# Strassen's seven products for pairs of up projections in a hybrid decoder trunk

## The chip, the cores and the metric

The kernel runs on one core of a Trainium2 chip. The metric is the device time of one execution in microseconds (us); lower is better. TensorE is called PE, its weight loads PEld, VectorE is DVE, ScalarE is ACT, GpSimd is POOL and SyncE is SP.

## What is computed

Two layers (`DEPTH`), 256 tokens, width 1024, hidden width 2816, float32. Each layer is

```python
x = x + 0.5 * swiglu(rmsnorm(x, norm_ffn1), w1, w3, w2)     # first FFN
h = rmsnorm(x, norm_mix); P = h @ w_in                       # the mixer: three branches, gates, one output
x = x + merged(retention, window attention, memory attention) @ w_o
x = x + 0.5 * swiglu(rmsnorm(x, norm_ffn2), w1, w3, w2)     # second FFN
...
def swiglu(h, w1, w3, w2):
    return (jax.nn.silu(h @ w1) * (h @ w3)) @ w2
```

and a final RMS norm. The memory attention projects `mem` (256 tokens, normed) in every layer, at the start of the mixer.

## The kernel before

**Matmuls in three passes.** Every large product is made from two-part operands: a value is split into a high part in the type fp32r and a low part, the rest. `three_passes` (L442 to L444) issues low x high, high x high and high x low into one PSUM bank, each with a stationary tile of 128 activations x 128 tokens and 512 moving columns of weight.

**Weights.** All large weights come from HBM as a stream of 1 MB units of 128x2048, in the order of use; 123 units per layer: 33 for each FFN, 57 for the mixer. A unit of an up projection holds a block of 512 of K by 512 columns (256 of w1 and 256 of w3 of one chunk). SP loads a unit into one of three buffers of `raw` (L356) after DVE has made the low part of the unit before in that buffer. ACT copies it to `w_hi` (`split`, L784) once PE has used the unit three places earlier; DVE subtracts into `w_lo` (`split`, L1054). The first two units are loaded and split in eight pieces of 512 columns (L347, L789, L1059).

**An FFN** (`ffn`) runs over 11 chunks of 256 hidden columns. A chunk has two up units (`project`, one for each half of K, 24 matmuls each: 4 blocks of K x 2 token tiles x 3 passes). ACT then makes `act_s`, the silu of the w1 half (L829), DVE multiplies the w3 half into `act_g` (L1100), PE transposes it (`gt`, L497), ACT and DVE make `gT_hi` and `gT_lo` (L795, L1065), and one down unit (24 matmuls) adds to four PSUM banks. The order on PE is up (first half) of the next chunk, transposes of this one, up (second half), down. The norm's factor `rstd` is applied in silu and gate product, so PE starts with unnormed x, transposed by PE and times the gains: `hi_parts` (ACT, L800) and `lo_parts` (DVE, L1071) make `hT_hi` and `hT_lo`. The second half of x is transposed inside the first up unit. `act_x_squares` (L776) and POOL (L374, L376) make `rstd`.

**The start.** The first 256 columns of x (part 0) are issued by SP, part 1 by ACT (L768, behind two small tables), part 2 by SP after the first unit's pieces. PE runs warm-up matmuls on zeros (L433) between the first transposes; `first_unit` then goes block of K by block of K.

**Order.** Each engine has one in-order list of instructions, written out by hand and tied by semaphores. `plan_banks` numbers the uses of the eight PSUM banks. The memory input is loaded twice in every layer, at the first chunk of the first FFN: transposed (`memT`, L835, split into `bT_hi` and `bT_lo` at L846 and L1121) and as it is (`stB`, L836, for its squares). The mixer's first unit stands ahead of the first FFN's last down unit.

Of the kernel before, what the change touches and what calls it, by code (L numbers as in the profile page):

```python
# [44 lines left out]
RING = 3  # L45

# [16 lines left out]
assert NU % RING == 0 and MIX_AT % RING == 0 and FFN2_AT % RING == 0  # L63
# [23 lines left out]

FFN_ENDS = [u in (1, FFN_UNITS - 1) or (1 < u and u % RING == 0) for u in range(FFN_UNITS)]
ENDS = FFN_ENDS + [last for *_, last in UNITS] + FFN_ENDS
ENDS[FIRST_MIX], ENDS[LAST_DOWN] = ENDS[LAST_DOWN], ENDS[FIRST_MIX]  # L90
USED = [ENDS[:u + 1].count(False) for u in range(NU)]
# [24 lines left out]
def plan_banks():  # L116
# [4 lines left out]
    def ffn(f):  # L121
        for t in range(TT):
            banks.add(f"up{f}_0t{t}", 2 + t)
            banks.add(f"up{f}t{t}", 4 + t, NCH - 1)
        banks.add(f"gt{f}", 6, NCH, split=True)
        for h in range(2):
            for t in range(TT):
                banks.add(f"down{f}_{h}{t}", 2 * h + t)
# [33 lines left out]
    xt("y1", 6)  # L162
# [4 lines left out]
def build(nc, x_in, mem_in, memt_in, stream, gains_in, gfin_in, rot_in, decay_in, mask_in, ident_in, out):  # L167
    banks = plan_banks()
    where, USES, HIS = banks.at, banks.uses, banks.hi

    ctx = ExitStack()
    with ctx:
# [19 lines left out]
        bT_hi = new("bT_hi", [P, KT, SEQ], F32R)  # L192
        bT_lo = new("bT_lo", [P, KT, SEQ], F32R)
# [6 lines left out]
        mkT = new("mkT", [P, KT, MEM])  # L200
# [7 lines left out]
        merged = new("merged", [P, TT, D], at=v_at)  # L208
        srg, s_at = place("srg", [P, TT, D])
        mpT = new("mpT", [P, MEM_H, TT, SEQ], at=s_at)  # L210
        sqT, sq_at = place("sqT", [P, KT, SEQ])
        gates = new("gates", [P, TT, D], at=sq_at)
        skT = new("skT", [P, SWA_KV, SEQ])
# [43 lines left out]

        raw_loaded = [sem(f"raw_loaded{s}") for s in range(RING)]
        hi_split, lo_split, unit_used = sem("hi_split"), sem("lo_split"), sem("unit_used")
# [13 lines left out]
        silu_ready = [sem(f"silu_ready{t}") for t in range(TT)]  # L273
# [26 lines left out]
        def used(l, unit):  # L300

            if not ENDS[unit]:
                return unit_used, l * USED[-1] + USED[unit]
            if unit < MIX_AT or unit >= FFN2_AT:
                f, at = (1, 0) if unit < MIX_AT else (2, FFN2_AT)
                if unit - at == FFN_UNITS - 1:
                    return full(l, f"down{f}_11")
                if unit - at == 1:
                    return full(l, f"up{f}_0t1")
                return full(l, f"up{f}t1", (unit - at) // RING - 1)  # L310
            if unit == LAST_DOWN:
                return full(l, "down1_11")
            return full(l, UNITS[unit - MIX_AT][0] + "t1")
# [24 lines left out]
        def _(sp):  # L338
# [11 lines left out]
            for u in range(EARLY, DEPTH * NU):  # L350
                s = u % RING
                if u >= RING + EARLY:
                    sp.wait_ge(lo_split, u - RING - EARLY + 1)
                elif u >= RING:
                    sp.wait_ge(first_lo, (u - RING + 1) * SUBS)
                sp.dma_start(raw[:, s], stream[u]).then_inc(raw_loaded[s], 16)  # L356
# [69 lines left out]
        def _(pe):  # L426
# [12 lines left out]
            def three_passes(dst, xh, xl, slot, cols, first, last):  # L439

                a, b = cols
                nc.tensor.matmul(dst, xl, w_hi[:, slot, a:b], start=first, stop=False)  # L442
                nc.tensor.matmul(dst, xh, w_hi[:, slot, a:b], start=False, stop=False)  # L443
                return nc.tensor.matmul(dst, xh, w_lo[:, slot, a:b], start=False, stop=last)  # L444
# [4 lines left out]
            def project(l, unit, names, hi, lo, half, c=0, inside=None, pairs=None):  # L449


                early = l == 0 and unit < EARLY
                if not early:
                    pe.wait_ge(lo_split, l * NU + unit - EARLY + 1)
                for t in range(TT):
                    if t == 1 and inside:
                        inside()
                    if half == 0:
                        pe.wait_ge(*room(l, names[t], c))
                    for j in range(UB):  # L460
# [3 lines left out]
                        if early and t == 0:  # L464
                            pe.wait_ge(first_lo, unit * SUBS + j + 1)
                        last = three_passes(bank(names[t])[:, :], hi[:, k, tokens(t)], lo[:, k, tokens(t)],
                                            unit % RING, (j * BLK, (j + 1) * BLK), k == 0, k == KT - 1)
# [5 lines left out]
            def project_kv(l, unit, names):  # L473

                pe.wait_ge(lo_split, l * NU + unit - EARLY + 1)
                for t in range(TT):
                    pe.wait_ge(*room(l, names[t]))
                    for k in range(KT):
                        last = three_passes(bank(names[t])[:, 0:256], hT_hi[:, k, tokens(t)], hT_lo[:, k, tokens(t)],
                                            unit % RING, (k * 256, (k + 1) * 256), k == 0, k == KT - 1)  # L480
# [43 lines left out]
            def ffn(l, f, at):  # L524
                up0, up = ([f"up{f}{of}t{t}" for t in range(TT)] for of in ("_0", ""))
                end = f == 2 and l == DEPTH - 1

                def transpose_g(c):
                    for t in range(TT):
# [3 lines left out]
                def down(c, unit, parts, inside=None):  # L533
# [5 lines left out]
                    for n, (h, t) in enumerate(parts):  # L539
# [3 lines left out]
                        if first:  # L543
                            pe.wait_ge(*room(l, name))
# [846 lines left out]
```

## Time and profile before

| | us |
|---|---|
| Median of three runs (lowest to highest) | 1515.35 (1514.86 to 1515.44) |
| The profiled execution's own time | 1514.35 |
| Its span, first to last instruction | 1512.4 |
| PE busy | 1499.4 |
| DVE busy | 795.0 |
| ACT busy | 739.3 |
| Mean granted clock of TensorE | 0.997 of full |

The time of an execution holds about 2 us around the span. Matmul records overlap (they are pipelined), so a matmul's share of the time is read from the distance between starts.

### The profile page before, as it was taken

How to read it: one execution, taken by the hardware profiler on the slowest of the kernel's cores; microseconds unless marked ns; L12 is line 12 of the kernel's file. 1: busy time of each engine (PE TensorE's matmuls, PEld its weight loads, DVE VectorE, ACT ScalarE, POOL GpSimd, SP SyncE). 2: the span in 40 equal slices, each digit the busy share in tenths (PEclk: the TensorE clock that was granted, in tenths of full speed). 3: DMA queues.
4: the chain of work that ended last, by engine and by line, in shares of the span. 5: the costliest groups of instructions: out<-in, count | busy, mean ns of one | idle time of the engine just before them, and what ended most of it. 6: DMA issues, size and time to landing. Idle time of an engine off the chain costs nothing.

```text
span 1512.4 us, 16913 instructions
## 1 busy us (share of the span) xinstructions
PE 1499.4 (99%) x7126; PEld 1246.7 (82%) x7126; DVE 795.0 (53%) x728; ACT 739.3 (49%) x903; POOL 56.5 (4%) x64
## 2 busy tenths in 40 slices
PE   8999999999999999999999999999999999999998
PEld 6888888888888888888888888888888888888886
DVE  5554554564555465455465455546545464655544
ACT  5544454655445435444364444556644544454443
POOL 0000000220000000000000000004100000000000
PEclk9999999999999999999999999999999999999999
DMA  8655555433453445555465555543444534555551
GB/s 299 231 194 195 173 189 173 161 140 140 141 193 140 167 173 189 189 176 192 169 250 193 184 183 190 189 169 143 140 147 160 192 143 151 196 179 186 192 195 55
DMA packets 39290, 266.89 MB, mean 176 GB/s; under 512 B 4432, under 2 KB 5072, under 8 KB 7728
## 3 DMA queue, kind: packets, MB, share of 16 engines
q1 hardware_dynamic: 37120, 259.28, 48.5%
q10 hardware_dynamic: 1824, 5.63, 1.0%
q8 instruction: 56, 0.92, 0.2%
q0 software_dynamic: 272, 0.92, 0.2%
q14 instruction: 18, 0.15, 0.0%
HBM read 264.76 MB, written 1.05 MB: 176 GB/s over the span
## 4 chain that ended last, share of the span: by engine, by line
PE 97%; ACT 1%; DVE 1%; DMA 1%; issue 0%; ACTq 0%; POOLq 0%; POOL 0%; DVEq 0%
PE bank L442 29%; PE bank L444 29%; PE bank L443 29%; PE bank L497 4%; PE bank L636 1%; PE bank L729 1%; PE bank L712 1%; PE bank L622 1%; PE bank L610 1%; DMA x<-in_x 1%; ACT w_hi L784 0%; ACT prob L969 0%; PE bank L634 0%; DVE w_lo L1054 0%; PE bank L684 0%; PE bank L694 0%
## 5 line engine op out<-in xcount | busy, mean ns | idle before, releaser
L1054 DVE TENSOR_TENSOR w_lo<-raw,w_hi 128x2048 fp32r<-128x2048 f32 x244 | 561.7, 2302 | 555.5 <-ACT w_hi L784 554.9
L784 ACT ACTIVATE w_hi<-raw 128x2048 fp32r<-128x2048 f32 x244 | 466.7, 1913 | 351.9 <-PE bank L444 348.2
L442 PE MATMUL bank<-w_hi,hT_lo 128*128 128x512 f32 (+1 forms) x1312 | 517.0, 394 | 0.5 <-issue 0.2
L444 PE MATMUL bank<-w_lo,hT_hi 128*128 128x512 f32 (+1 forms) x1312 | 508.5, 388 | 0.0
L443 PE MATMUL bank<-w_hi,hT_hi 128*128 128x512 f32 (+1 forms) x1312 | 507.7, 387 | 0.0
L442 PEld LDWEIGHTS bank<-w_hi,hT_lo 128*128 128x128 f32 x1312 | 246.8, 188 | 51.7 <-issue 4.4
L444 PEld LDWEIGHTS bank<-w_lo,hT_hi 128*128 128x128 f32 x1312 | 246.5, 188 | 51.3
L443 PEld LDWEIGHTS bank<-w_hi,hT_hi 128*128 128x128 f32 x1312 | 247.0, 188 | 47.6
L442 PE MATMUL bank<-w_hi,gT_lo 128*128 128x512 f32 x352 | 137.4, 390 | 0.2
L444 PE MATMUL bank<-w_lo,gT_hi 128*128 128x512 f32 x352 | 137.0, 389 | 0.0
L443 PE MATMUL bank<-w_hi,gT_hi 128*128 128x512 f32 x352 | 137.0, 389 | 0.0
L442 PE MATMUL bank<-w_hi,bT_lo 128*128 128x512 f32 x320 | 126.4, 395 | 0.0
L444 PE MATMUL bank<-w_lo,bT_hi 128*128 128x512 f32 x320 | 124.7, 390 | 0.0
L443 PE MATMUL bank<-w_hi,bT_hi 128*128 128x512 f32 x320 | 124.6, 389 | 0.0
L795 ACT ACTIVATE gT_hi<-bank 128x512 fp32r<-128x512 f32 x44 | 26.3, 598 | 158.6 <-PE bank L497 158.6
L829 ACT ACTIVATE act_s<-bank,rstd 128x256 f32<-128x256 f32 x88 | 41.7, 475 | 104.3 <-PE bank L444 104.2
L1065 DVE TENSOR_TENSOR gT_lo<-bank,gT_hi 128x512 fp32r<-128x512 f32 x44 | 30.4, 692 | 92.9 <-ACT gT_hi L795 92.9
L442 PEld LDWEIGHTS bank<-w_hi,gT_lo 128*128 128x128 f32 x352 | 66.1, 188 | 14.6 <-issue 1.0
L444 PEld LDWEIGHTS bank<-w_lo,gT_hi 128*128 128x128 f32 x352 | 66.1, 188 | 13.8
L443 PEld LDWEIGHTS bank<-w_hi,gT_hi 128*128 128x128 f32 x352 | 66.1, 188 | 13.5
L444 PEld LDWEIGHTS bank<-w_lo,bT_hi 128*128 128x128 f32 x320 | 60.1, 188 | 12.6
L442 PEld LDWEIGHTS bank<-w_hi,bT_lo 128*128 128x128 f32 x320 | 60.1, 188 | 12.6 <-issue 0.7
(134 smaller groups left out, 916.9 us busy)
## 6 DMA issues: line engine op xcount, KB each, us to landing
raw<-in_stream SPq DMA_DIRECT2D x244, 1024.0 KB, 4.9
raw<-in_stream SPq DMA_DIRECT2D x8, 256.0 KB, 7.7
memT<-in_memt ACTq DMA_DIRECT2D x2, 1024.0 KB, 7.7
stB<-in_mem ACTq DMA_DIRECT2D x2, 1024.0 KB, 15.3
x<-in_x SPq DMA_DIRECT2D x1, 512.0 KB, 8.5
decay<-in_decay POOLq DMA_DIRECT2D x1, 512.0 KB, 10.3
gfin<-in_gfin ACTq DMA_DIRECT2D x1, 512.0 KB, 4.5
out<-stB ACTq DMA_DIRECT2D x2, 256.0 KB, 2.3
```

The lines of the kernel that those rows point to most:

```text
L442: nc.tensor.matmul(dst, xl, w_hi[:, slot, a:b], start=first, stop=False)
L443: nc.tensor.matmul(dst, xh, w_hi[:, slot, a:b], start=False, stop=False)
L444: return nc.tensor.matmul(dst, xh, w_lo[:, slot, a:b], start=False, stop=last)
L497: last = nc.tensor.transpose(bank(name)[:, at:at + P], src(t, k0 + j), ident[:, :])
L610: last = nc.tensor.matmul(bank(name)[:, i * n:(i + 1) * n], sqT[rows, head // 2, tokens(b)], skT[rows, head // (SWA_H // SWA_KV), 0:n], st ...
L622: last = nc.tensor.transpose(bank(name)[:, i * P:(i + 1) * P], prob[:, g % 2, head, col:col + P], ident[:, :])
L636: last = nc.tensor.matmul(o[:, HD:2 * HD], pT[:, GRP + 2 * i + t, :], v[t], start=t == 0, stop=t == TT - 1)
L784: nc.scalar.activation(w_hi[:, s], raw[:, s], ACT.Copy).then_inc(hi_split, 1)
L795: nc.scalar.activation(dst[:, k0:k0 + 2, :].rearrange("p k t -> p (k t)"), bank(name)[:, :], ACT.Copy).then_inc(hisem(name), 1)
L829: nc.scalar.activation(act_s[:, t, :], bank(up)[:, 0:FC], ACT.Silu, scale=rstd[:, t:t + 1]).then_inc(silu_ready[t], 1)
L1054: nc.vector.tensor_tensor(w_lo[:, s], raw[:, s], w_hi[:, s].bitcast(F32), ALU.subtract).then_inc(lo_split, 1)
L1065: nc.vector.tensor_tensor(lo[:, k0:k0 + 2, :].rearrange("p k t -> p (k t)"), bank(name)[:, :], hi[:, k0:k0 + 2, :].bitcast(F32).rearrange( ...
```

## The change

In every FFN, chunks 3 and 4 and chunks 6 and 7 are made as pairs. The left matrix h is cut into quarters by token tile and half of K, the right one by half of K and chunk; seven products (Winograd's form) replace eight. Products 1, 2 and 4 take quarters of `hT_hi`/`hT_lo` as they are; 5, 6, 7 and 3 take the four sums of quarters in `S_hi`/`S_lo`. Products 1, 3 and 2 take a weight block as it is (11, 22, 21); 5, 6, 7 and 4 take four sums of weight blocks, made by DVE in place in the raw buffers. Which operand is which stands in `WEIGHT`, `SUMS` and `product` below. Some additions of products happen by accumulation in a PSUM bank: 6, 7 and 4 go on in bank 7 where product 1 stands, 3 in bank 5 where product 5 stands. ACT keeps copies (`snap`) of banks after products 1, 5 and 3, and DVE adds them to the bank after products 2, 6 and 7 (`half`).

The order on PE (`ffn_steps`) puts other work between the products. For an FFN it is: up 0, up 1 (first half), gt 0, up 1, down 0, up 2, gt 1, up 2, down 1, then product 1, gt 2, product 5, down 2, products 3 and 6, up 5 (first half), product 7, up 5, gt 4, product 4, down 4, gt 5, product 2; then product 1 of the second pair, down 5, gt 3, product 5, down 3, product 3, up 8, product 6, up 8, product 7, gt 8, up 9, product 4, up 9, down 8, gt 7, product 2, down 7, gt 9, up 10, down 9, gt 6, up 10, down 6, gt 10, (mixer's first unit), down 10.

A split weight is now an item: 135 in a layer instead of 123. In the FFNs there are four slots of `w_hi`/`w_lo` and seven raw buffers, the extra ones in memory that the mixer's tiles hold at other times; the splits of item o + 4 are issued after item o. The sums of quarters need h as plain float32: ACT copies the transposed blocks from PSUM to `hF` (`copies`), DVE those of the first half in the first FFN. The sums stand on DVE behind the second item's splits (the first FFN) or the first item's (the others). x's part 1 moves to SP's queue behind the first weight piece. The start's dummy activation takes the function Silu instead of Copy. `memT` is loaded after the last pair's products, `stB` two items of PE later, and the memory's squares come at the mixer's first unit.

```diff
+SEGMENTS = {1: [(0,),(1,),(2,),(3,4,5),(6,7,8,9),(10,)],
+            2: [(0,),(1,),(2,),(3,4,5),(6,7,8,9),(10,)]}
+WEIGHT = {1: "11", 5: "11", 3: "22", 6: "11", 7: "12", 4: "11", 2: "21"}
+SUMS = {1: ("11", "12", "11"), 2: ("11", "22", "11"), 3: ("12", "22", "12"), 4: ("11", "21", "11")}
+SUM_OF = {5: 1, 6: 2, 7: 3, 4: 4}
+NEEDS = {1: ("11", "12"), 3: ("22",), 7: ("21",)}
...
# plan_banks
+            elif s[0] == "prod":
+                banks.add("p{1}_{2}_{3}".format(*s), {5: 5, 3: 5, 2: 4}.get(s[3], 7))
...
# SP
                     sp.dma_start(raw[:, u, cols], stream[u, :, cols]).then_inc(first_raw[u * SUBS + j], 16)
+                    if (u, j) == (0, 0):
+                        x_part(1)
...
+            for o, unit, s, (until, owner) in loads[EARLY:]:
+                if until > 0:
+                    sp.wait_ge(weights_made, until)
...
+                if s >= RING and ITEMS[o % NI][1] == 2 and (owner is None or ...):
+                    sp.wait_ge(*full(o // NI, "mg1_1"))
+                sp.dma_start(raw_slot(s), stream[unit]).then_inc(raw_loaded[s], 16)
...
# PE
+                def product(k, n):
+                    name, o = f"p{f}_{k}_{n}", l * NI + AT["prod", f, k, n]
+                    left = {1: (0, 0), 2: (0, 1), 4: (1, 1)}
+                    pe.wait_ge(*lo_ready(o))
+                    pe.wait_ge(*room(l, name))
+                    if n == 5:
+                        pe.wait_ge(S_lo_split, 2 * at_f + 1)
+                    elif n == 3:
+                        pe.wait_ge(S_lo_split, 2 * at_f + 2)
+                    for j in range(UB):
+                        if n in left:
+                            t, h = left[n]
+                            xh, xl = (v[:, UB * h + j, tokens(t)] for v in (hT_hi, hT_lo))
+                        else:
+                            m = {5: 0, 6: 1, 7: 2, 3: 3}[n]
+                            xh, xl = (v[:, m, j, :] for v in (S_hi, S_lo))
+                        last = three_passes(bank(name)[:, :], xh, xl, o, (j * BLK, (j + 1) * BLK),
+                                            n in (1, 2, 5) and j == 0, j == UB - 1, n in (6, 7, 4, 3))
+                    last.then_inc(fullsem(name), 1)
...
# ACT
-            act.dma_start(x[:, :, X_PARTS[1]], x_in[...]).then_inc(x_loaded[1], 16)
-            nc.scalar.activation(junk[:, 0, 0:1], still[:, 0:1], ACT.Copy)
+            nc.scalar.activation(junk[:, 0, 0:1], still[:, 0:1], ACT.Silu)
...
+                    if s[0] == "up" and s[2:] == (0, 0):
+                        if f == 1 and l == 0:
+                            for j in range(UB):
+                                first_split(j)
+                                if j < 2:
+                                    hi_parts(0, f"x0_{j}", hT_hi, 2 * j, gain)
+                        else:
+                            copies(0)
+                        for j in range(2):
+                            hi_parts(l, f"{xy}1_{j}", hT_hi, UB + 2 * j, gain)
+                        if f == 1 and l == 0:
+                            for j in range(SUBS, PIECES):
+                                first_split(j)
+                            split(EARLY)
+                        copies(1)
+                        if f == 1 and l == 0:
+                            act_x_squares(0, 0)
...
+                        if s[3] in (1, 5, 3):
+                            act.wait_ge(*full(l, name))
+                            nc.scalar.activation(snap[s[3]][:, :], bank(name)[:, :], ACT.Copy).then_inc(free(name), 1)
...
# DVE
+            def split(o):
+                (hi, lo), (s, _) = slots(o), loaded(o)
+                for pair, k in sums_first[o]:
+                    to, plus, minus = (raw_of[o // NI, pair, q] for q in SUMS[k])
+                    dve.wait_ge(raw_loaded[plus[0]], 16 * plus[1])
+                    nc.vector.tensor_tensor(raw_slot(to[0]), raw_slot(plus[0]), raw_slot(minus[0]), ALU.subtract)...
+                dve.wait_ge(hi_split, o - EARLY + 1)
+                nc.vector.tensor_tensor(lo, raw_slot(s), hi.bitcast(F32), ALU.subtract).then_inc(weights_made, 1)
...
+                        if m in half:
+                            other = {2: 1, 6: 3, 7: 5}[m]
...
+                            nc.vector.tensor_tensor(half[m][:, :], bank(name)[:, :], snap[other][:, :], ALU.add)\
+                                .then_inc(free(name), 1)
...
+                def later(s):
+                    if s == S_STEPS[at_f][0]:
+                        left_sums()
+                    if s == S_STEPS[at_f][2]:
+                        left_parts()
```

`left_sums` is four f32 additions or subtractions of 128x512 on DVE, `left_parts` the two low splits of their results; ACT makes the high parts between them.

## Rows read from the trace of the kernel before

**Rows 1.** The page, its first part: span, then busy time by engine

```profile
span 1512.4 us, 16913 instructions
PE 1499.4 (99%) x7126; PEld 1246.7 (82%) x7126; DVE 795.0 (53%) x728; ACT 739.3 (49%) x903; POOL 56.5 (4%) x64
```

**Rows 2.** The page, the chain that ended last, by engine

```profile
PE 97%; ACT 1%; DVE 1%; DMA 1%; issue 0%; ACTq 0%; POOLq 0%; POOL 0%; DVEq 0%
```

**Rows 3.** Waits of PE: waiting line, what for, total us, times, longest

```profile
PE bank L497 <- DMA x<-in_x: 2.8, 1, 2.8
PE bank L622 <- DVE prob L1212: 0.4, 2, 0.2
```

**Rows 4.** Busy time by windows, one chunk of the first FFN, from transposes to transposes

```profile
63.85:80.64 16.79, 16.79 (x77) 13.90 (x76) 8.45 (x6) 7.08 (x6) 0.00 (x0) 1.00 0.54 189
```

**Rows 5.** The page, costliest groups: count | busy us, mean ns | idle before

```profile
L1054 DVE TENSOR_TENSOR w_lo<-raw,w_hi 128x2048 fp32r<-128x2048 f32 x244 | 561.7, 2302 | 555.5 <-ACT w_hi L784 554.9
L784 ACT ACTIVATE w_hi<-raw 128x2048 fp32r<-128x2048 f32 x244 | 466.7, 1913 | 351.9 <-PE bank L444 348.2
L443 PE MATMUL bank<-w_hi,hT_hi 128*128 128x512 f32 (+1 forms) x1312 | 507.7, 387 | 0.0
...
L829 ACT ACTIVATE act_s<-bank,rstd 128x256 f32<-128x256 f32 x88 | 41.7, 475 | 104.3 <-PE bank L444 104.2
L1065 DVE TENSOR_TENSOR gT_lo<-bank,gT_hi 128x512 fp32r<-128x512 f32 x44 | 30.4, 692 | 92.9 <-ACT gT_hi L795 92.9
```

**Rows 6.** Groups by line and shape, operations like those that are added

```profile
L923 ACT ACTIVATE pT<-bank 128x512 f32<-128x512 f32 x24 | 12.4, 593 | 0.0
...
L1100 DVE SCALAR_TENSOR_TENSOR act_g<-bank,rstd,act_s 128x256 f32<-128x256 f32 x88 | 42.0, 481 | 34.8 <-ACT act_s L829 34.7
...
L1186 DVE TENSOR_TENSOR merged<-merged,gates 128x512 f32<-128x512 f32 x16 | 11.1, 692 | 0.6
```

**Rows 7.** The chain in order of time, the start: start us, us, what

```profile
1.74 8.07 DMA x<-in_x
...
12.26 0.43 PE bank L442
...
13.38 0.23 PE bank L442
...
30.39 0.44 PE bank L497 x4
```

**Rows 8.** Timeline of the start: start us, us, engine, instruction, idle before

```profile
5.98 0.63 ACT L789 ACTIVATE w_hi<-raw 128x512 fp32r<-128x512 f32 x1 [2.25 <-DMA gains<-in_gains]
...
8.63 0.63 ACT L789 ACTIVATE w_hi<-raw 128x512 fp32r<-128x512 f32 x1 [1.29 <-DMA raw<-in_stream]
...
15.94 1.57 ACT L800 ACTIVATE hT_hi<-bank,gains 128x256 fp32r<-128x256 f32 x4 [3.05 <-PE bank L497]
...
23.36 1.92 ACT L784 ACTIVATE w_hi<-raw 128x2048 fp32r<-128x2048 f32 x1
...
23.89 0.71 POOL L376 TENSOR_TENSOR rstd<-rstd,mhalf 128x2 f32<-128x2 f32 x1
```

**Rows 9.** Timeline of layer 1's first FFN, its first up unit

```profile
757.78 1.57 ACT L800 ACTIVATE hT_hi<-bank,gains 128x256 fp32r<-128x256 f32 x4 [5.69 <-PE bank L497]
...
762.52 1.03 PE L497 MATMUL bank<-ident,x 128*128 128x128 f32 x8
763.15 1.57 ACT L800 ACTIVATE hT_hi<-bank,gains 128x256 fp32r<-128x256 f32 x4 [2.00 <-PE bank L497]
764.03 1.66 DVE L1071 SCALAR_TENSOR_TENSOR hT_lo<-bank,gains,hT_hi 128x256 fp32r<-128x256 f32 x4 [0.55 <-ACT hT_hi L800]
```

**Rows 10.** The page, DMA issues: KB each, median us from issue to landing

```profile
raw<-in_stream SPq DMA_DIRECT2D x244, 1024.0 KB, 4.9
...
memT<-in_memt ACTq DMA_DIRECT2D x2, 1024.0 KB, 7.7
stB<-in_mem ACTq DMA_DIRECT2D x2, 1024.0 KB, 15.3
```

More of the change, by code:

```diff
@@ L86 @@
 FIRST_MIX, LAST_DOWN = MIX_AT - 1, MIX_AT
[L88 to L91, printed above, removed]
+SEGMENTS = {1: [(0,),(1,),(2,),(3,4,5),(6,7,8,9),(10,)],
+            2: [(0,),(1,),(2,),(3,4,5),(6,7,8,9),(10,)]}
+PAIRS = {f: [seg for seg in SEGMENTS[f] if len(seg) > 1] for f in (1, 2)}
@@ new lines, with unit_of @@
+USED = [sum(s[0] == "up" and s[3] == 0 or s[0] == "down" and s[2] != DOWNS[s[1]][-1]
+            or s[0] == "mix" and not UNITS[s[1]][2] and UNITS[s[1]][0] != "skv" for s in ITEMS[:i + 1]) for i in range(NI)]
+def unit_of(s):
+    if s[0] == "mix":
+        return FIRST_MIX if s[1] == 0 else MIX_AT + s[1]
+    at = 0 if s[1] == 1 else FFN2_AT
+    if s[0] == "up":
+        return at + s[3] if s[2] == 0 else at + 3 * s[2] - 1 + s[3]
+    if s[2] < NCH - 1:
+        return at + 4 + 3 * s[2]
+    return LAST_DOWN if s[1] == 1 else NU - 1
@@ L437, in _, with three_passes, project @@
             pe.wait_ge(ident_loaded, 16)
[L439 to L444, printed above, removed]
+            def three_passes(dst, xh, xl, o, cols, first, last, more=False):
+                (wh, wl), (a, b) = slots(o), cols
+                nc.tensor.matmul(dst, xl, wh[:, a:b], start=first, stop=False, skip_group_check=more)
+                nc.tensor.matmul(dst, xh, wh[:, a:b], start=False, stop=False, skip_group_check=more)
+                return nc.tensor.matmul(dst, xh, wl[:, a:b], start=False, stop=last, skip_group_check=more)
             def tokens(t):
                 return slice(t * P, (t + 1) * P)
[L449 to L454, printed above, removed]
+            def project(l, i, names, hi, lo, half, inside=None, pairs=None):
+                o = l * NI + i
+                if o >= EARLY:
+                    pe.wait_ge(*lo_ready(o))
                 for t in range(TT):
@@ L522, in first_unit, with ffn @@
                 last.then_inc(unit_used, 1)
[L524 to L525 removed]
+            def ffn(l, f):
                 end = f == 2 and l == DEPTH - 1
[L528 to L552 removed]
+                xy, at_f = "xy"[f - 1], ffn_no(l, f)
+                order = DOWNS[f]
                 by_half = [(h, t) for h in range(2) for t in range(TT)]
@@ new lines, in down @@
+                def down(c, parts, inside=None):
+                    first, last_chunk, o = c == order[0], c == order[-1], l * NI + AT["down", f, c]
+                    pe.wait_ge(*lo_ready(o))
+                    pe.wait_ge(*out_of(l, f"gt{f}_{c}"))
+                    g_hi, g_lo = gT[order.index(c) % 2]
+                    for n, (h, t) in enumerate(parts):
+                        if inside and n == len(parts) - 1:
+                            inside()
+                        name = f"down{f}_{h}{t}"
+                        if first:
+                            pe.wait_ge(*room(l, name))
+                        for j in range(2):
+                            i = three_passes(bank(name)[:, :], g_hi[:, j, tokens(t)], g_lo[:, j, tokens(t)],
+                                             o, ((2 * h + j) * BLK, (2 * h + j + 1) * BLK),
+                                             first and j == 0, last_chunk and j == 1)
+                        if last_chunk:
+                            i.then_inc(fullsem(name), 1)
+                    if not last_chunk:
+                        i.then_inc(unit_used, 1)
```

630 lines of the change are left out of this document (416 added, 214 removed).

## The prediction

> **What bounds the kernel now.** I read the page from the top. TensorE is busy 1499.4 of 1512.4 us, VectorE (DVE) and ScalarE (ACT) about half [rows 1]. The chain that ended last lies on PE for 97%, nearly all of it in the three lines of `three_passes` [rows 2]. PE's waits come to some 5 us in all, the longest the 2.8 us for a part of x at the start [rows 3]. So what is taken from PE's instruction count is worth its full price, as long as the two engines that make the weights' high and low parts keep up. The reader should look next at one whole chunk of an FFN: 16.79 us, PE busy for all of it at full clock, DVE 8.45 and ACT 7.08 [rows 4]. It holds three weight units of 24 matmuls and four transposes. The transposes take 0.44 us, so a matmul of 512 columns is worth (16.79 - 0.44)/72 = 0.227 us; the 387 to 390 ns of a matmul's own row [rows 5] overlap and are not what one costs. A unit is 5.45 us.
>
> **What is removed.** Two chunks' up projections are four units, 96 matmuls: eight products of (128 tokens x 512 of K) by a 512x512 weight block, 12 matmuls each. A pair now takes seven, 84 matmuls. Eight pairs (two in each of four FFNs) save 96 matmuls: 96 x 0.227 = 21.8 us. Products take the same tiles and the same shape, and the additions of products happen in the PSUM banks or on DVE, so nothing is added to PE. The Trainium skill (TensorE: Matmul & The Clock Gate, "Wait — 56ns, not 53.3ns?") gives 215.7 ns from start to start for 512 columns on a warm array; by that the saving would be an estimated 20.7 us. The trace's spacing is 227 ns and decides.
>
> **What is added on DVE and ACT.** Before, one 2.30 us low split (DVE) and one 1.91 us high split (ACT) served 5.45 us of PE. A product has its own weight for 2.73 us only, and four of seven weights are sums, each another 128x2048 subtract on DVE. No such f32 result stands in the trace. Below it the nearest is w_lo itself, 2.30 [rows 5]; above, four all-SBUF f32 subtracts of 512 columns, 4 x 0.69 = 2.77 [rows 6]. I take 2.30, the row of the same shape.
>
> Take the tightest stretch, the first pair of an FFN with what is woven between: products 1, 5, 3, 6, 7, 4, 2, two up units and downs 2 and 4, and three gT transposes. PE: 7 x 2.73 + 4 x 5.45 + 3 x 0.44 = 42.2. DVE in it (splits are made four items ahead): 11 splits 25.3, three sums 6.9, three gT_lo 2.1, six gate products of 0.48 and three additions of a product to its snapshot of 0.69, 5.0 together [rows 5, 6]: 39.3, that is 93%. ACT: 11 x 1.91 + 3 snapshots and 3 gT_hi of 0.6 + six silus of 0.48 = 27.5. The second pair has three more full units between: PE 58.6, DVE about 47. So by totals PE stays the bound. By latency the tightest place is product 7, which writes bank 7 after DVE has read product 6 there: from the end of down 2, ACT's high split 1.9, DVE low split, sum, low split 6.9, the addition 0.7, together 9.5; PE meanwhile has products 3 and 6 and an up unit, 10.9. Margin 1.4 per pair, and 0.9 with sums at 2.77. I take no cost there; its cover is that margin, and if a sum costs more than 3.7 it is gone.
>
> Snapshots (0.6 on ACT, as pT from PSUM [rows 6]) free banks long before their next product. The eight extra copies of h's blocks from PSUM in each FFN lie beside PE except at the two places below. SP issues the same 252 weight loads into seven raw buffers in place of three; a load waits for splits, and in the stretch above each is still issued more than 10 us ahead of its split, against 4.9 us to land [rows 10]. The loads into buffers that the mixer used wait for `mg1`'s transposes, some 27 us before their unit is due.
>
> **The start.** Part 1 of x was issued on ACT's queue at 1.74 beside the weight pieces and landed at 9.81; PE idled for it, then transposed, warmed and began at 12.26, its first matmuls 0.43 apart, later 0.23 [rows 7]. The first weight piece was in use at 5.98 and the second at 8.63 [rows 8]. Now this part is third in SP's queue, ahead of the second piece. Two transfers in 3.8 us, 1.9 each: it lands near 7.9. The bounds are no gain and the 2.8 us idle; I take 2.2, between the 1.9 of even shares and the 2.8. It pushes all later weight pieces back 0.5 of issue, which their splits, queued behind ACT's copies, hide.
>
> **What comes back.** In layer 0, ACT has four more copies before the squares (1.5). Squares ended at 23.36; now 23.36 - 2.2 + 1.5 = 22.7, rstd 23.9 [rows 8], high split of unit 3 by 24.6. DVE then runs in order: low split 3 to 26.9, the two gate products to 27.8, low splits 4 and 5 to 32.2, four sums of h (0.65 each) to 34.8, and only then gT_lo of chunk 0, to 35.5. PE ends unit 1 at 22.7 (30.39 - 5.45 - 2.2 [rows 7]), unit 2 at 28.2, transposes, ends unit 3 at 34.1 and wants gT for down 0: it waits 1.4. Bounds 0 to 3; I take 1.5.
>
> In layer 1, x's second half: today x1's transposes start at 762.5 and ACT takes them at 763.15, DVE at 764.0 [rows 9]. Now two splits of 1.85 and four copies 1.5 stand on ACT after the first half's parts (759.35), to 764.6; DVE's two low splits end at 765.7 and the first low pair at 766.5, where PE wants it at 765.9: 0.6 later. For the second FFNs the same sum ends 0.3 us ahead of PE: nothing.
>
> memT's load and parts now come after the last pair. Counted from the pair's last product: load issued near 8.4, landing 7.7 later [rows 10], ACT's eight parts to 23.2, DVE's to 26.5, gate products to 27.4, and PE wants these at 28.2 and memT at 28.6. No cost, a margin of 0.8. The early Silu table load hides in the start's idle time. The end is untouched.
>
> **Sum.** Against the profiled execution's own 1514.35: - 21.8 - 2.2 + 1.5 + 0.6 = - 21.9, so 1492.4. The median of the runs, 1515.35, is 1.0 above the profiled one: 1493.5.
>
> **Rivals.**
> 1. DVE loses a little in each pair: handovers between ACT's and DVE's in-order queues (a sum has to end before ACT's high split of its weight can begin, and DVE sits behind that) eat the 1.4 us margin and 1 us more. For it: DVE already waits 554.9 us for w_hi [rows 5], and 93% of a stretch leaves 2.9 us. Against: the four items of lead. Eight pairs by 1 us: about 1501.5. Chance 0.18.
> 2. memT lands late and holds ACT and DVE in front of chunk 10's gates. With 15.3 us to land, as the memory's other load took [rows 10], ACT starts 3.8 late and PE waits 3.0, in two layers: 1499.5. Chance 0.06; it was loaded against more traffic than it will meet.
> 3. Slower: sums. Each of the 32 weight sums writes the raw buffer that it reads, while ACT and DMA work in its neighbours. If that doubled its price to 4.6, each would put 4.6 - 3.7 = 0.9 on the path and the total of the first stretch (46.2) would pass PE's too: 32 x 0.9 = 29 us, 1493.5 + 29 = 1522. It decides from 3.7 + 21.9/32 = 4.4 us a sum. No all-SBUF row hints at it [rows 6]. Chance 0.05.
> 4. The start's wait for gT_lo does not arise, or all of the x wait goes: 1490.7. Chance 0.10.
> 5. The clock. After 2.8 us of waiting PE's first matmuls ran at the lower level, 0.43 apart [rows 7]. A 1.5 us wait at down 0 could do so again: a handful at 0.2 more, 1 to 2 us: 1495. No row here has a wait of this length in the middle. The Trainium skill (TensorE: Matmul & The Clock Gate, Part 1) says that the array falls back to 1.2 GHz after it has idled. Chance 0.06.
> 6. The seven products do not save: PE would have to be slower per matmul in products. All operands have today's shapes. Chance 0.02, no change.
>
> **How the numbers follow.** Forecast 0.53, the rest as above. The range: 1490 takes in rival 4, 1502 rivals 1, 2 and 5; out stay rivals 3 and 6 and a rest. A measurement can tell 0.2% (3 us) from no change. Faster 0.92, same 0.03, slower 0.05.
>
> **What would show it.** The changed profile should have each of the three matmul lines 32 fewer (96 in all), the same 0.227 spacing inside products, w_lo splits up from 244 to 268 (seven weights in place of four in each of eight pairs), and 32 sums near 2.3 us. The timeline should show down 0 of layer 0 waiting about 1.5 us for gT_lo and no PE idle over 0.3 us inside a pair. Stretch by stretch, DVE should be near 90% in the first pair. Wrong: PE idle before product 7 or 5 in each pair (rival 1, or 3 if the sums' rows are long), before chunk 10's transposes (rival 2), or a first matmul still at 12.

## The result, and the profile after

The changed kernel took 1491.47 us (median of four runs, 1491.36 to 1491.57) against 1515.11 us for the kernel before, measured beside it (four runs, 1512.56 to 1515.44): a ratio of 0.9848, with a 95% interval of 0.9835 to 0.986. That is 23.6 us by the medians and 22.7 by the spans of the profiled executions. Forecast were 1493.5, 21.9 less, in a range of 1490 to 1502.

The page's first part and the chain by engine of the changed kernel, which answer to [rows 1, 2]:

```profile
span 1489.7 us, 17013 instructions
PE 1477.1 (99%) x7030; PEld 1227.0 (82%) x7030; DVE 946.5 (64%) x836; ACT 814.5 (55%) x986; POOL 56.9 (4%) x64
...
PE 95%; ACT 2%; DVE 1%; DMA 1%; issue 1%; SPq 0%; POOLq 0%; POOL 0%; ACTq 0%; DVEq 0%
```

PE has 96 instructions fewer and is busy 22.3 us less, which is nearly all of the 22.7 us that the span lost. DVE carries 151.5 us more and is still on 1% of the chain only.

Groups by line and shape of the changed kernel, what was added to DVE and ACT (count, busy us, mean ns, idle before):

```profile
L1343 DVE TENSOR_TENSOR w_lo<-raw,w_hi 128x2048 fp32r<-128x2048 f32 x164 | 378.0, 2305 | 382.6 <-ACT w_hi L1028 381.9
...
L1104 ACT ACTIVATE snap<-bank 128x512 f32<-128x512 f32 x24 | 14.3, 598 | 11.3 <-PE bank L646 11.3
...
L1341 DVE TENSOR_TENSOR raw_more<-raw_more 128x2048 f32<-128x2048 f32 x10 | 22.8, 2284 | 0.0
L1341 DVE TENSOR_TENSOR raw<-raw_more,raw 128x2048 f32<-128x2048 f32 x9 | 20.6, 2285 | 0.0
L1341 DVE TENSOR_TENSOR raw_more<-raw,raw_more 128x2048 f32<-128x2048 f32 x9 | 20.6, 2284 | 0.0
L1441 DVE TENSOR_TENSOR half<-bank,snap 128x512 f32<-128x512 f32 x24 | 16.4, 684 | 0.0
...
L1341 DVE TENSOR_TENSOR raw<-raw 128x2048 f32<-128x2048 f32 x4 | 9.1, 2283 | 0.0
```

A weight sum, which writes the buffer that it reads, takes 2.284 us, a shade under a split. The four forms make 32, and the splits with the three other forms of the same group (x64, x21, x19) 268.

Waits of PE, the whole run of the changed kernel, against [rows 3]:

```profile
PE bank L635 <- POOL still L569: 2.0, 1, 2.0
PE bank L644 <- issue: 1.6, 3, 1.3
PE bank L644 <- DVE hT_lo L1366: 0.6, 2, 0.3
PE bank L700 <- DVE act_g L1386: 0.5, 1, 0.5
PE bank L861 <- DVE prob L1551: 0.4, 2, 0.2
```

The 2.8 us for x are gone. None of these waits lies in a pair, as the busy time by windows shows: around down 0 of layer 0 (33 to 36), in the first pair's stretch, and in the second's. The columns are length, then PE, PEld, DVE, ACT and POOL busy, granted clock, DMA share, GB/s:

```profile
33.00:36.00 3.00, 1.74 (x8) 1.33 (x8) 3.00 (x4) 2.22 (x3) 0.00 (x0) 1.00 1.01 415
59.60:101.70 42.10, 42.10 (x193) 34.92 (x192) 36.42 (x25) 26.32 (x22) 0.00 (x0) 1.00 0.58 214
101.70:160.30 58.60, 58.60 (x265) 48.49 (x265) 45.39 (x33) 33.26 (x28) 0.00 (x0) 1.00 0.50 180
```

Both pairs' stretches have PE busy for their whole length, 42.1 and 58.6 us, as summed.

**Where the time went**, by laying matching places of the two timelines side by side (start of the same transposes, before and after, us from the span's start):

| place | before | after | gained since the place above |
|---|---|---|---|
| chunk 1's transposes, layer 0 | 47.04 | 45.42 | 1.6: the start |
| the mixer's first, layer 0 | 206.91 | 199.86 | 5.4: two pairs |
| the second FFN's first, layer 0 | 568.76 | 561.70 | 0.0: the mixer |
| layer 1's first | 757.14 | 744.65 | 5.4: two pairs |
| the second FFN's first, layer 1 | 1315.50 | 1298.20 | 4.8: two pairs less 0.6 |
| end of the span | 1512.4 | 1489.7 | 5.4: two pairs |

A pair of 12 matmuls at 0.227 is 2.7, two are 5.4. The 0.6 in layer 1 is the wait for `hT_lo`: PE's idle time there is listed as 0.34, but the distance between the starts around it is 0.73 where 0.23 is usual, because a matmul's record of 0.39 reaches beyond the start of the next, 0.23 later. For the same reason the wait of 1.26 at down 0 costs 1.5 and the wait of 0.55 for `act_g` 0.7 (0.93 between starts).

### The profile page after: what moved, and what is told of

The parts are those of the page before. It is cut to its first block, busy times and chain, and to the rows that moved or that the text cites. A ratio compares the mean times of both kernels' runs of the same rounds, so it can differ in the third digit from the quotient of the medians.

```text
span 1489.7 us, 17013 instructions
## 1 busy us (share of the span) xinstructions
PE 1477.1 (99%) x7030; PEld 1227.0 (82%) x7030; DVE 946.5 (64%) x836; ACT 814.5 (55%) x986; POOL 56.9 (4%) x64
## 4 chain that ended last, share of the span: by engine, by line
PE 95%; ACT 2%; DVE 1%; DMA 1%; issue 1%; SPq 0%; POOLq 0%; POOL 0%; ACTq 0%; DVEq 0%
PE bank L644 29%; PE bank L646 28%; PE bank L645 28%; PE bank L700 4%; PE bank L875 1%; PE bank L968 1%; PE bank L951 1%; PE bank L861 1%; DMA raw<-in_stream 1%; ACT w_hi L1028 1%; PE bank L849 1%; ACT prob L1256 0%; DVE w_lo L1343 0%; PE bank L873 0%; SPq L546 0%
## 5 line engine op out<-in xcount | busy, mean ns | idle before, releaser
L1343 DVE TENSOR_TENSOR w_lo<-raw,w_hi 128x2048 fp32r<-128x2048 f32 x164 | 378.0, 2305 | 382.6 <-ACT w_hi L1028 381.9
L1028 ACT ACTIVATE w_hi<-raw 128x2048 fp32r<-128x2048 f32 x164 | 314.0, 1915 | 281.2 <-PE bank L646 263.0
L644 PE MATMUL bank<-w_hi,hT_lo 128*128 128x512 f32 (+1 forms) x1024 | 403.0, 394 | 1.1 <-DVE hT_lo L1366 0.6
L646 PE MATMUL bank<-w_lo,hT_hi 128*128 128x512 f32 (+1 forms) x1024 | 396.0, 387 | 0.0
L645 PE MATMUL bank<-w_hi,hT_hi 128*128 128x512 f32 (+1 forms) x1024 | 395.4, 386 | 0.0
L644 PEld LDWEIGHTS bank<-w_hi,hT_lo 128*128 128x128 f32 x1024 | 192.5, 188 | 42.6 <-issue 4.8
L645 PEld LDWEIGHTS bank<-w_hi,hT_hi 128*128 128x128 f32 x1024 | 192.7, 188 | 36.5
L1343 DVE TENSOR_TENSOR w_lo<-raw_more,w_hi 128x2048 fp32r<-128x2048 f32 x64 | 146.1, 2289 | 38.0 <-ACT w_hi L1028 37.9
L1028 ACT ACTIVATE w_hi<-raw_more 128x2048 fp32r<-128x2048 f32 x64 | 122.6, 1918 | 33.3 <-PE bank L646 32.5
L1045 ACT ACTIVATE gT_hi<-bank 128x512 fp32r<-128x512 f32 x44 | 26.4, 600 | 100.8 <-PE bank L700 100.8
L645 PEld LDWEIGHTS bank<-w_hi,bT_hi 128*128 128x128 f32 x320 | 60.2, 188 | 11.8
```

The costliest lines, as they stand in the source:

```text
L644: nc.tensor.matmul(dst, xl, wh[:, a:b], start=first, stop=False, skip_group_check=more)
L645: nc.tensor.matmul(dst, xh, wh[:, a:b], start=False, stop=False, skip_group_check=more)
L646: return nc.tensor.matmul(dst, xh, wl[:, a:b], start=False, stop=last, skip_group_check=more)
L1028: nc.scalar.activation(slots(o)[0], raw_slot(s), ACT.Copy).then_inc(hi_split, 1)
L1045: nc.scalar.activation(dst[:, k0:k0 + 2, :].rearrange("p k t -> p (k t)"), bank(name)[:, :], ACT.Copy).then_inc(hisem(name), 1)
L1343: nc.vector.tensor_tensor(lo, raw_slot(s), hi.bitcast(F32), ALU.subtract).then_inc(weights_made, 1)
```

## Experiments

All are edits of the changed kernel unless said otherwise. Where one execution alone is given, a difference of some tenths of a us is not read from its time. The kernel before took 1514.59 (seven runs) beside the kernels with x on ACT's queue, with the sums of h later, with sums longer by half and with the second pair only; 1515.38 (one run) beside those with sums more than doubled, three pairs and three slots; and 1514.38 (13 runs, on another chip) beside the last two.

### x's part 1 back on ACT's queue

```diff
-                    if (u, j) == (0, 0):
-                        x_part(1)
...
+            act.dma_start(x[:, :, X_PARTS[1]], x_in[...]).then_inc(x_loaded[1], 16)
```

> The changed kernel with one part undone: x's part 1 is issued on ACT's queue again, as before. Theory (the start is gained by the order of transfers): the part lands near 9.8 us again instead of before 6.85, x's last transposes fall back from 11.5 to about 15.3, and with them ACT's copies, the squares, rstd and DVE's list up to gT_lo of chunk 0. Everything after is 3 us later: 1494.5. Rival (the load of weight unit 2, landing at 16.4, sets ACT's list at the start, so x's part is worth only what lies beyond it): ACT's list is bound by x only from 17.4 on, 1.0 to 1.5 later than now: about 1492.8.

Measured: 1494.78 (1494.57 to 1495.95), 3.3 above the changed kernel, ratio to before 0.9869 (0.9855 to 0.9884). PE's timeline at the start, from the slowest of the four executions (1495.95; the others took 1494.57 to 1494.84):

```profile
10.39 1.12 PE L698 MATMUL bank<-ident,x 128*128 128x128 f32 x4 [3.83 <-DMA x<-in_x]
...
12.23 0.99 PE L642 MATMUL bank<-w_hi,hT_lo 128*128 128x512 f32 x1
13.01 0.63 PE L643 MATMUL bank<-w_hi,hT_hi 128*128 128x512 f32 x1
```

The same rows of the changed kernel:

```profile
6.85 0.66 PE L700 MATMUL bank<-ident,x 128*128 128x128 f32 x4
...
8.39 0.50 PE L644 MATMUL bank<-w_hi,hT_lo 128*128 128x512 f32 x1 [0.23 <-DVE hT_lo L1366]
8.73 0.40 PE L645 MATMUL bank<-w_hi,hT_hi 128*128 128x512 f32 x1
```

With the part on SP's queue PE transposes it 3.5 us earlier and starts the first product 3.8 us earlier, with records of 0.40 in place of 0.63. The granted clock was 0.50 from 10 to 15 us in this kernel, behind the wait of 3.83, and 1.00 from 5 to 10 in the changed one, which has no such wait. That one line of the diff is worth 3.3 us by the medians.

### The four sums of h one item later in the first FFN

```diff
-S_STEPS = [[ITEMS[AT["up", n % 2 + 1, 0, 0] + (n == 0) + i] for i in range(3)] ...
+S_STEPS = [[ITEMS[AT["up", n % 2 + 1, 0, 0] + 2 * (n == 0) + i] for i in range(3)] ...
```

> The changed kernel with the four sums of h's quarters in the very first FFN one item later in DVE's list (behind gT_lo of chunk 0 instead of in front of it), their high and low parts one item later too. Theory: the 1.3 us that PE waits before down 0 at 33.2 us goes, and nothing takes its place, because product 5 comes 14 us after the parts are made: 1490.2, no PE wait between 28 and 200 us. Rival: the sums' 2.7 us move the wait to down 1 or product 5: 1491.5 as now.

In the changed kernel DVE and PE met at down 0 of layer 0 like this (timeline of DVE, then the row of PE from its own timeline):

```profile
26.73 4.48 DVE L1343 TENSOR_TENSOR w_lo<-raw_more,w_hi 128x2048 fp32r<-128x2048 f32 x2
31.14 0.68 DVE L1394 TENSOR_TENSOR S_sum<-hF 128x512 f32<-128x512 f32 x1
...
33.66 0.68 DVE L1360 TENSOR_TENSOR gT_lo<-bank,gT_hi 128x512 fp32r<-128x512 f32 x1
```

```profile
32.80 0.39 PE L646 MATMUL bank<-w_lo_more,hT_hi 128*128 128x512 f32 x1
34.45 0.47 PE L644 MATMUL bank<-w_hi,gT_lo 128*128 128x512 f32 x1 [1.26 <-issue]
...
34.99 0.39 PE L646 MATMUL bank<-w_lo,gT_hi 128*128 128x512 f32 x1
35.22 0.39 PE L644 MATMUL bank<-w_hi,gT_lo 128*128 128x512 f32 x1
```

The wait is labelled "issue", but down 0 begins 0.1 us after `gT_lo` ends at 34.34, and that is its real releaser. Measured with the sums behind it: 1489.85 (1489.27 to 1490.33), ratio 0.9835 (0.9818 to 0.9851), 1.6 less than the changed kernel. The wait at down 0 is gone and none took its place; the one of 0.55 for `act_g` before chunk 0's transposes is still there. This is the fastest kernel of the study.

### Each weight sum made longer by half

Two scratch subtractions of 128x512 stand before each of the 32 sums (they are extra work; nothing is left out). Each pair of them takes 1.41 us, and starts 1.3 us before the sum, so a sum costs in effect 3.6 to 3.7.

```diff
+                    for _ in range(2):
+                        nc.vector.tensor_tensor(spare[:, :], x[:, 0, 0:BLK], x[:, 1, 0:BLK], ALU.subtract)
                     nc.vector.tensor_tensor(raw_slot(to[0]), ...
```

> Two more DVE subtractions of 128x512 (scratch, no part of the result) in front of each of the 32 weight sums: a sum costs 2.28 + 1.3 = about 3.6 instead of 2.28. The prediction's margin (product 7 behind product 6 only, free up to 3.7) expects no cost: 1491.5 to 1492. The rival reading walks DVE's list item by item: gT_lo of chunk 2 stands behind a sum and two splits and PE wants it for down 2 sooner than product 7 wants its bank; it expects PE waits of about 2.5 at down 2, 0.7 at product 7 and 1 at the transposes of chunk 8 in every FFN, 17 us in all: 1505 to 1510.

Measured in one execution: 1500.68, 9.2 more than the changed kernel. Its waits of PE, its DVE's timeline and its PE's:

```profile
PE bank L646 <- DVE gT_lo L1370: 7.1, 4, 1.8
```

```profile
58.27 1.41 DVE L1350 TENSOR_TENSOR spare<-x 128x512 f32<-128x512 f32 x2
59.59 2.28 DVE L1351 TENSOR_TENSOR raw<-raw_more,raw 128x2048 f32<-128x2048 f32 x1
61.80 2.28 DVE L1353 TENSOR_TENSOR w_lo_more<-raw_more,w_hi_more 128x2048 fp32r<-128x2048 f32 x1
64.00 0.69 DVE L1370 TENSOR_TENSOR gT_lo<-bank,gT_hi 128x512 fp32r<-128x512 f32 x1
```

```profile
64.83 0.47 PE L646 MATMUL bank<-w_hi,gT_lo 128*128 128x512 f32 x1 [1.78 <-DVE gT_lo L1370]
```

The same place of the changed kernel:

```profile
56.76 2.28 DVE L1341 TENSOR_TENSOR raw<-raw_more,raw 128x2048 f32<-128x2048 f32 x1
59.01 2.29 DVE L1343 TENSOR_TENSOR w_lo_more<-raw_more,w_hi_more 128x2048 fp32r<-128x2048 f32 x1
61.21 0.68 DVE L1360 TENSOR_TENSOR gT_lo<-bank,gT_hi 128x512 fp32r<-128x512 f32 x1
```

```profile
62.70 0.39 PE L644 MATMUL bank<-w_hi,gT_lo 128*128 128x512 f32 x1
```

There `gT_lo` of chunk 2 ends at 61.89 and down 2 takes it at 62.70: a margin of 0.8 us. Two sums of the first pair stand ahead of it on DVE (the earlier one at 47.3), so two surcharges of 1.3 push it by 2.6, and 2.6 - 0.8 is the wait of 1.8. It comes once per FFN, and by the matching places each FFN takes 2.2 us longer, which makes 9.0 of the 9.2. (The wait of 0.8 for x that this execution had at the start left 0.2 by chunk 1's transposes, 45.60 against 45.42.) No product waits. The cost is real but about half of the 17 us that the walk through the queues had given, because the later places kept more slack than walked. The place of the wait is what counts: not the one that the prediction called tightest.

### Each weight sum more than doubled

As before with four scratch subtractions, 128 in all, 88.3 us of DVE or 2.8 for each sum, which brings it to 4.9 to 5.1.

```diff
-                    for _ in range(2):
+                    for _ in range(4):
```

> Four scratch subtractions of 128x512 on DVE in front of each of the 32 weight sums: a sum costs 2.28 + 2.6 = 4.9. The prediction's rival 3 (free to 3.7, then each of 32 on the path) gives 32 x 1.2 = 38: 1530. The walk of DVE's list gives first waits of about 5 at down 2 (gT_lo of chunk 2), then 3 at product 7 of the first pair and 4.7 of the second: 14 a FFN, 57 in all; but it had 17 for the half price and 9 were measured, so some 45: 1535 to 1545. In both, slower than the kernel before.

Measured in one execution: 1550.87, 59 more than the changed kernel and 35 more than the kernel before. Waits of PE, and two windows, one in the first and one in the second pair's stretch:

```profile
PE bank L646 <- DVE half L1451: 20.2, 8, 3.7
PE bank L646 <- DVE gT_lo L1370: 18.7, 4, 4.7
```

```profile
62.00:80.00 18.00, 13.32 (x53) 10.60 (x52) 17.86 (x14) 8.52 (x6) 0.00 (x0) 0.91 0.34 122
125.00:150.00 25.00, 21.34 (x86) 17.21 (x85) 24.60 (x21) 10.48 (x10) 0.00 (x0) 0.86 0.70 252
```

Now DVE is full and the addition `half` of a product to its snapshot waits in it too, twice per FFN. The listed waits come to 38.9 of the 59 us. The granted clock falls to 0.91 and 0.86 in these windows (0.983 over the run against 0.999), so the waits cost again in slower matmuls afterwards. The rival "slower" of the prediction exists, at a price half as high again as its formula gives.

### Only the second pair of each FFN

```diff
-SEGMENTS = {1: [(0,),(1,),(2,),(3,4,5),(6,7,8,9),(10,)],
-            2: [(0,),(1,),(2,),(3,4,5),(6,7,8,9),(10,)]}
+SEGMENTS = {1: [(0,),(1,),(2,),(3,),(4,),(5,),(6,7,8,9),(10,)],
+            2: [(0,),(1,),(2,),(3,),(4,),(5,),(6,7,8,9),(10,)]}
```

> One pair per FFN (chunks 6 and 7) instead of two; chunks 3, 4 and 5 are made the plain way, with the same lists of slots and loads. Theory (a pair is worth its 12 matmuls, nothing else): four times 12 x 0.227 = 10.9 us more: 1502.4, 48 matmuls more, and 12 splits and 16 sums fewer. Rival (the first pair, where DVE is at 87%, costs hidden waits or slower matmuls): less than 10 us more.

Measured in one execution: 1503.24, 11.8 more. Four pairs are 48 matmuls, 10.9 us. The other 0.9 is a wait before chunk 10's transposes in layer 0's first FFN:

```profile
PE bank L700 <- DVE act_g L1386: 0.9, 2, 0.7
```

The longer of the two, 0.69, ends at 189.38; the last matmul before it starts at 188.30, so 1.08 lie between starts where 0.23 is usual. DVE made memT's low parts (`bT_lo`) from 185.24 to 188.49, and the gate product behind them ended at 189.28. (The wait of 1.2 for x at this execution's start left only 0.06 by chunk 1's transposes, 45.48 against 45.42.) From the second FFN's first transposes to layer 1's first it takes 185.71 in place of 182.95, 2.8 more, where no such wait lies. A first pair is worth its 12 matmuls, 2.7, though DVE is busy for 87% of it; the second pair has 77%.

### Three pairs in an FFN

Chunks 1 and 2, 4 and 5, 7 and 8. The sums of h are one item earlier, and PE waits for the copies of h before the first product.

```diff
+SEGMENTS = {1: [(0,),(1,2,3),(4,5,6),(7,8,9),(10,)],
+            2: [(0,),(1,2,3),(4,5,6),(7,8,9),(10,)]}
-S_STEPS = [[ITEMS[AT["up", n % 2 + 1, 0, 0] + (n == 0) + i] for i in range(3)] ...
+S_STEPS = [[ITEMS[AT["up", n % 2 + 1, 0, 0] + i] for i in range(3)] ...
...
+                    if at_f == 0 and (k, n) == (0, 1):
+                        pe.wait_ge(x0_copied, 2)
```

> A third pair in every FFN: chunks 1 and 2, 4 and 5, 7 and 8 as pairs, 3, 6, 9 woven in, 0 and 10 alone. The first product now follows chunk 0's up units directly, so the sums of h's quarters stand one item earlier in the first FFN too. Theory by counts (PE is the bound, pairs of three chunks fit since DVE is at 87% in one): 48 matmuls fewer, 1491.5 - 10.9 = 1480.6. Rival, walking DVE's and ACT's lists: inside the pairs PE still does not wait, but product 5 comes some 8 us after chunk 0 while the sums of h's quarters and their parts need copies, splits and four sums first; PE waits 8 to 11 us for S_lo and 1 to 3 us for chunk 0's gates in every FFN, and 3 to 4 for memT's parts in both layers: about 1525 to 1530, slower than the kernel before.

Measured in one execution: 1568.22, slower than the kernel before by 53, with 48 matmuls fewer than the changed kernel. The largest waits of PE, and two windows:

```profile
PE bank L644 <- DVE S_lo L1406: 29.5, 4, 8.8
PE bank L644 <- DVE hT_lo L1368: 12.6, 3, 4.6
PE bank L644 <- DVE half L1443: 11.0, 4, 2.8
PE bank L700 <- DVE act_g L1388: 6.9, 1, 6.9
```

```profile
32.00:45.00 13.00, 4.19 (x12) 3.14 (x13) 13.00 (x8) 3.75 (x4) 0.00 (x0) 0.50 0.24 84
60.00:100.00 40.00, 40.00 (x184) 33.11 (x183) 35.22 (x26) 23.09 (x22) 0.00 (x0) 1.00 0.47 165
```

Once such an FFN runs, its pairs are smooth (60 to 100: PE busy throughout, and no wait until 178). What doesn't fit is, first, the pair at the FFN's start: its product 5 needs the sums of h, which need all of h, and DVE has the pair's own weight sums at the same time. The waits for `S_lo`, `hT_lo` and chunk 0's `act_g` are 49 of the 64 us that PE waited for DVE. PE waits up to 8.8 us and then works at half the clock. Second, at the FFN's end the last pair's addition `half` holds PE for 2.8 in all four, and memT's parts (`bT_lo`) add 4.2 in the whole run. The direction was expected, the size was some 40 us short: the walk had not found the waits for `hT_lo` and `half` (23.6 us), and had no term for the lower clock (0.976 over the run).

### Three slots of split weights in place of four

```diff
-        s = min(range(RING + of_ffn(o)), key=lambda v: last[v])
+        s = min(range(RING), key=lambda v: last[v])
```

> The changed kernel with three slots of split weights in the FFNs instead of four (a split is issued three items ahead). Theory (the fourth slot is what lets DVE run behind the two-thirds of a unit that a product leaves it): several us of PE waits in every pair, over 1500. Rival (by the walk of the lists the lead of three items still covers ACT's 1.9 and DVE's 2.3 or 4.6): 0.7 before down 5 and some tenths at two transposes in each FFN, 3 to 4 us in all, less the 1.3 us wait of the first FFN's down 0: 1493 to 1495.

Measured in one execution: 1491.93, 0.5 more. PE waits four times 0.3 us for `w_lo`, and the wait at down 0 is gone, so the fair comparison is the kernel with the sums of h later (1489.85), which lacks that wait too: 2.1 more. By matching places an FFN takes 0.6 to 0.7 us longer. The theory, that the fourth slot carries the pairs, is wrong: it buys about 0.6 us in each FFN.

### The kernel before with the new start alone

The kernel before, with x's part 1 third in SP's queue and the dummy activation as Silu.

```diff
+                    if (u, j) == (0, 0):
+                        x_part(1)
...
-            act.dma_start(x[:, :, X_PARTS[1]], x_in[...]).then_inc(x_loaded[1], 16)
-            nc.scalar.activation(junk[:, 0, 0:1], still[:, 0:1], ACT.Copy)
+            nc.scalar.activation(junk[:, 0, 0:1], still[:, 0:1], ACT.Silu)
```

> The kernel before with two parts of the change alone: x's part 1 in SP's queue behind the first weight piece, and the start's dummy activation with the function Silu. No products, no sums. Theory: PE's first real matmuls come 3 to 4 us sooner and nothing gives it back, since the four copies and the sums of h that cost a wait in the changed kernel are not there: 3.3 us (what undoing it cost the changed kernel) below the kernel before, about 1511.5. Rival: with three raw buffers the third unit's load (it lands near 16) and unit 3's split bind, and half is lost: 1513 to 1513.5.

Measured: 1510.65 (1510.02 to 1511.27), ratio 0.9976 (0.9967 to 0.9986): 3.7 less. In the traces chunk 1's transposes start at 43.19 for 47.04, 3.85 sooner, and the changed kernel has them at 45.42: what the products bring with them (the copies and sums of h) gives 2.2 of the start back, 1.5 at down 0 and 0.7 at chunk 0's transposes. So the start and the products share the gain as 3.7 and 1510.65 - 1491.47 = 19.2 (these two not measured beside each other). With the sums of h moved behind `gT_lo` the products give 20.8 of their 21.8: that kernel took 1489.85, and so did the kernel of the next section, which was measured beside this one.

The new start also narrows the spread: ten executions lie within 1.3 us here, 13 of the kernel before within 3.5 (1512.42 to 1515.94). Its fastest gains only 2.4.

### The dummy activation back to Copy

On the kernel with the sums of h later.

```diff
-            nc.scalar.activation(junk[:, 0, 0:1], still[:, 0:1], ACT.Silu)
+            nc.scalar.activation(junk[:, 0, 0:1], still[:, 0:1], ACT.Copy)
```

> The kernel with the sums one item later (1489.85) with the start's dummy activation put back to the function Copy, so that ACT loads the table for Silu when the first silu is due. Theory: the first gates are on the path by 0.5 us (PE waited for act_g), so a table load of 1.28 between rstd and the first silu costs 1.3: 1491.1. Rival: the load slips into ACT's wait for rstd and costs nothing: 1489.9.

Measured: 1489.85 (1489.22 to 1490.36), the same as without the edit. The rival was right on the time but not on the reason. The load does not slip into a wait; it stands between a high split and the first silu:

```profile
22.89 1.28 ACT L1072 ACT_TABLE_LOAD   x1
```

The silus follow at 24.18 and end at 25.02. DVE has a low split from 22.90 to 25.19 ahead of the gate products that use them, so by this trace PE doesn't wait for the load. As far as four runs on each side show, this line of the diff is worth nothing, and the 3.7 us of the start belong to x's place in the queue.

## Why the prediction was right, point by point

**What is removed: right.** 96 matmuls at 0.227 us, 21.8. The matching places give two pairs' worth per FFN, 5.4, and the first pair's 12 matmuls were measured alone by leaving it out. The trace's spacing decided: the estimate of 20.7 from the Trainium skill (TensorE: Matmul & The Clock Gate, "Wait — 56ns, not 53.3ns?") would ask for 0.216 in place of the 0.23 between starts here too (34.99 and 35.22 behind down 0's wait, above).

**What is added: prices right, cover right, its weak place wrong.** A sum took 2.284 us for 2.30, a snapshot 0.598 for 0.6; DVE's 36.4 us in the first stretch (87%) stand against 39.3 (93%), ACT's 26.3 against 27.5, DVE's 45.4 against 47 in the second. (The window holds 25 DVE operations where 26 were summed, and neighbouring records overlap by up to 0.1.) Rival 1 is out: no PE wait in a pair. But "by latency the tightest place is product 7", with a margin of 1.4, "and if a sum costs more than 3.7 it is gone" was wrong. The tightest place is `gT_lo` of chunk 2 before down 2, behind a sum and two splits in DVE's list: its margin is 0.8, with two sums ahead of it, so the cover ends near 2.28 + 0.8/2, some 2.7 us a sum. The prediction looked for the place among the products alone. It did not hurt, since the real sum is at 2.28; with the bound of 2.77 it would have cost some 0.2 in four places. For the same reason rival 3's line, free to 3.7 and level with before at 4.4, was off at its start and too gentle: at 3.7 a sum cost 9.2 us in all, at 4.9 it cost 59 where the formula gives 32 x 1.2 = 38. The lower clock after the long waits is part of that gap. The crossing with the kernel before lies between the two prices; no run shows where.

**The start: right in kind, too small.** Forecast were 2.2 us for x's part; the measured worth is 3.3 (taken back alone) to 3.7 (put in alone). The landing was not far off: PE takes the part at 6.85 in the trace above and between 7.0 and 8.1 in the eight other kernels with the new order, where 7.9 was summed from even shares of the first transfers. What failed is the bound "the 2.8 us idle". It counted the wait alone and left out that behind the wait PE's first matmuls had run 0.43 apart [rows 7], while they now run 0.23 apart almost from the first.

**What comes back: right in what it named, one term short.** The wait at down 0 for `gT_lo` came as computed, 1.5 by the distance between starts for 1.5, and its cause is shown by moving the four sums (1.6 less). In layer 1, 0.6 came for 0.6. Missing is the 0.7 at chunk 0's transposes for `act_g`: the prediction had the gate products done at 27.8 and PE there at 28.2, so 0.4 to spare. They were done at 26.82, but PE, which had gained more at the start than forecast, was there at about 26.4. Of rival 4, which named two things, the second came true (all of x's wait went) and the first did not (the wait for `gT_lo` arose). What was not seen ahead either is that unit 2's load, which lands at 16.43, now heads the chain that leads to this place; it, and no longer x, sets when ACT comes to the squares. `memT` cost nothing in the changed kernel, and rival 2 is out; but its margin is thin, for the kernel with the second pair only lost 0.9 behind memT's parts, before chunk 10's transposes, the place that the prediction named.

```profile
memT<-in_memt ACTq DMA_DIRECT2D x2, 1024.0 KB, 4.8
stB<-in_mem ACTq DMA_DIRECT2D x2, 1024.0 KB, 5.9
```

Moved away from the start of an FFN, these loads land in 4.8 and 5.9 us, not in 7.7 and 15.3 [rows 10].

**The clock.** Rival 5 is out: across the 1.26 us wait the granted clock was 1.00, and the matmuls after it stand 0.23 apart. The Trainium skill (TensorE: Matmul & The Clock Gate, Part 1) has the array fall to 1.2 GHz after idling; the long waits of the two slow kernels (sums more than doubled, three pairs) agree with that, this short one did not bring it.

**Sum.** Forecast - 21.8 - 2.2 + 1.5 + 0.6 = - 21.9; measured in the traces, - 21.8 - 3.8 + 1.5 + 0.7 + 0.6 = - 22.8, against 22.7 by spans and 23.6 by medians. The start was 1.6 too small and the wait for `act_g` was missing; the two errors have opposite signs, and that the total came within 1 us owes something to luck. The other 1.0 between 1493.5 and 1491.47 is the amount by which the median of the kernel before lay above its profiled execution, and which the forecast added. The changed kernel has no such spread: its four runs lie within 0.2 us.

## What to carry to other kernels

When the bound engine's instructions are cut, count them by the spacing in the trace and then walk the helpers' in-order lists place by place. A helper's busy share over a stretch (87% here) doesn't show its weakest place, which can be an old small operation that now queues behind the new large ones; put those behind it, as the sums of h, or price the place by the number of new operations ahead of it. More of a good change can turn it round: three pairs ran smoothly in the middle of an FFN and lost it all at its two ends, most of it at the start. And look at the order of the first loads even when the change is about something else.

## What the runs showed of the hardware

- **The granted clock.** In the changed kernel it stayed at 1.00 across waits of 1.26 us, and with sums at 3.7 across waits of 1.8 us; with waits of 3.7 to 4.7 us it fell to 0.86 to 0.91 in the windows around them, and with waits up to 8.8 us to 0.50, that is 1.2 GHz for the whole window. A wait of 2.8 us was enough, too: at the start of the kernel before (0.50 from 10 to 13 us), and with three pairs in the middle of a busy stretch, where PE was busy without a break at 1.00 from 160 to 177.8, waited 2.76, took up its work at 180.93, and was granted 0.81 from 181 to 190. Matmul records are 0.63 at the lower level, as behind the 4.7 us wait with sums at 4.9:

```profile
67.20 0.77 PE L646 MATMUL bank<-w_hi,gT_lo 128*128 128x512 f32 x1 [4.68 <-DVE gT_lo L1370]
67.76 0.63 PE L647 MATMUL bank<-w_hi,gT_hi 128*128 128x512 f32 x1
```

- **POOL behind DVE.** In the kernel with three pairs the small power for `rstd` on POOL took 2.71 us, where it takes 0.70 at the same place of the changed kernel. It ended 0.6 us after a weight sum on DVE had, from the timeline:

```profile
21.74 2.28 DVE L1343 TENSOR_TENSOR raw<-raw_more,raw 128x2048 f32<-128x2048 f32 x1
21.88 2.71 POOL L578 TENSOR_TENSOR rstd<-rstd,mhalf 128x2 f32<-128x2 f32 x1
```

The Trainium skill (SBUF — State Buffer, "SBUF: two separate sides") says that a DVE operation with two SBUF inputs holds a port pair against a GpSimd operation that reads SBUF, for the whole instruction; this row agrees. No experiment was made on it alone.
